# A two-layer decoder trunk: first conditioning strips loaded by feature half, and half of the first projections ahead of the second half

## What is computed

```
mod = silu(c) @ w_ada[0] + b_ada[0]           # 1024 -> 6 x 1024: shift1, scale1, gate1, shift2, scale2, gate2
h   = x * (1 + scale1) + shift1
z   = h @ w_in[0]                             # columns: 256 c_q | 128 c_kv | 64 k_rope | 512 gate_b | 512 gate_c | 512 u
q, k, v from rms_norm(c_q), rms_norm(c_kv), rope -> causal attention (4 heads)
conv = gate_b * causal_conv3(gate_c * u)
y   = concat(rms_norm(attn), rms_norm(conv)) @ w_o[0]
x   = layer_norm(alpha * x + gate1 * y)
```

## Time and profile before

| | us |
|---|---|
| median of three runs | 1417.23 (1416.96 to 1418.35) |
| profiled execution, first to last instruction (its span) | 1415.7 |
| what the median has beside that span | 1.5 |
| PE busy | 1390.7 (98%) |
| DVE busy | 1251.7 (88%) |
| ACT busy | 1012.6 (72%) |
| DMA | 482.16 MB, mean 341 GB/s |

### The profile page before, as it was taken

One profiled execution on the slowest core, in us unless ns is written; L12 is line 12 of the kernel. 1 busy time (PEld: TensorE's weight loads), 2 busy tenths in 40 slices (PEclk: granted clock), 3 DMA queues, 4 the chain that ended last, 5 costly groups with the idle time before them and its releaser, 6 DMA issues.

```text
span 1415.7 us, 20150 instructions
## 1 busy us (share of the span) xinstructions
PE 1390.7 (98%) x7013; PEld 1149.1 (81%) x7013; DVE 1251.7 (88%) x1388; ACT 1012.6 (72%) x1286; POOL 63.3 (4%) x123
## 2 busy tenths in 40 slices
PE   6999999999999999999999999999999999999996
PEld 4876999997967888888888888888888888888885
DVE  5987888876799989998998899999889899899998
ACT  2453544454355888888988888888898888888884
POOL 1000000000013500000000000000000000001000
PEclk9999999999999999999999999999999999999998
DMA  9996398977564999999999999999999999999970
GB/s 361 416 412 240 143 349 290 378 282 276 207 258 171 385 369 366 392 380 375 379 393 365 366 398 367 380 383 387 367 379 392 365 371 392 387 362 390 413 306 32
DMA packets 203472, 482.16 MB, mean 341 GB/s; under 512 B 6944, under 2 KB 31630, under 8 KB 203418
## 3 DMA queue, kind: packets, MB, share of 16 engines
q1 hardware_dynamic: 198848, 470.31, 88.1%
q0 software_dynamic: 1584, 5.77, 1.0%
q10 hardware_dynamic: 2986, 5.38, 1.0%
HBM read 475.67 MB, written 5.77 MB: 340 GB/s over the span
## 4 chain that ended last, share of the span: by engine, by line
PE 96%; DVE 2%; DMA 1%; ACT 0%; issue 0%; POOL 0%; SPq 0%; ACTq 0%; DVEq 0%; POOLq 0%
PE ps L1794 27%; PE ps L1796 27%; PE ps L1795 27%; PE ps L1957 2%; PE ps L2144 2%; PE ps L1815 2%; PE ps L1918 2%; PE ps L1971 1%; PE ps L1756 1%; DMA raw<-in_w_ada_dram 1%; PE ps L1731 1%; PE ps L1867 0%; PE ps L2094 0%; PE ps L1773 0%; PE ps L1729 0%; PE ps L1898 0%
## 5 line engine op out<-in xcount | busy, mean ns | idle before, releaser
L1424 DVE TENSOR_TENSOR low<-raw,w_hi 128x1024 fp32r<-128x1024 f32 x448 | 531.6, 1218 | 24.4 <-ACT w_hi L853 16.2
L853 ACT ACTIVATE w_hi<-raw 128x1024 fp32r<-128x1024 f32 x448 | 470.2, 1061 | 84.3 <-PE ps L1796 79.4
L1795 PE MATMUL ps<-low,h_hi 128*128 128x512 f32 x904 | 351.9, 389 | 0.0
L1794 PE MATMUL ps<-w_hi,h_lo 128*128 128x512 f32 x680 | 269.5, 396 | 0.0
L1796 PE MATMUL ps<-w_hi,h_hi 128*128 128x512 f32 x680 | 265.3, 390 | 0.0
L1795 PE MATMUL ps<-low,hid_hi 128*128 128x512 f32 x528 | 205.7, 390 | 0.0
L1795 PEld LDWEIGHTS ps<-low,h_hi 128*128 128x128 f32 x904 | 169.9, 188 | 34.2
L1424 DVE TENSOR_TENSOR low<-raw,e_hi 128x1024 fp32r<-128x1024 f32 x112 | 136.7, 1220 | 19.8 <-ACT e_hi L853 19.8
L1796 PEld LDWEIGHTS ps<-w_hi,h_hi 128*128 128x128 f32 x680 | 127.6, 188 | 27.4
L1794 PEld LDWEIGHTS ps<-w_hi,h_lo 128*128 128x128 f32 x680 | 127.8, 188 | 24.9
L1424 DVE TENSOR_TENSOR low<-raw,hx_lo 128x1024 fp32r<-128x1024 f32 x112 | 136.5, 1219 | 3.7
(11 more groups left out here) (377 smaller groups left out, 2268.0 us busy)
## 6 DMA issues: line engine op xcount, KB each, us to landing
raw<-in_moe_w_gate_dram SPq DMA_DIRECT2D x56, 2048.0 KB, 8.5
raw<-in_moe_w_up_dram SPq DMA_DIRECT2D x56, 2048.0 KB, 8.6
raw<-in_moe_w_down_dram SPq DMA_DIRECT2D x56, 2048.0 KB, 8.7
raw<-in_w_ada_dram SPq DMA_DIRECT2D x20, 2048.0 KB, 12.7
raw<-in_w_in_dram SPq DMA_DIRECT2D x6, 2048.0 KB, 12.5
raw<-in_ffn_w_gate_dram SPq DMA_DIRECT2D x11, 1024.0 KB, 8.3
raw<-in_ffn_w_up_dram SPq DMA_DIRECT2D x11, 1024.0 KB, 10.9
raw<-in_ffn_w_down_dram SPq DMA_DIRECT2D x11, 1024.0 KB, 4.9
```

What stands on the lines that cost most here:

```text
L853: act.activation(e_hi[k % ERING], raw[moe_slot(m)][:, (k % 4) * UNIT:(k % 4 + 1) * UNIT], ACT.Copy).then_inc(unit_hi, 1)
L1424: dve.tensor_tensor(low[moe_slot(m)][:, part], raw[moe_slot(m)][:, part], e_hi[k % ERING].bitcast(F32), ALU.subtract).then_inc(unit_lo, 1)
L1794: pe.matmul(o, x_lo, hi, start=first, stop=False, skip_group_check=True)
L1795: pe.matmul(o, x_hi, lo, start=False, stop=False, skip_group_check=True)
```

## The change

1. **c from rows.** `c` was loaded as a column per partition with 1024 elements of 4 bytes. It is now 8 rows of 128, and the first 2048 values of `b_ada` are 16 more; PE turns the 24 rows at once, ACT takes the Silu and two bias tables from PSUM.
2. **Strips by feature half.** The first four strips now hold 512 rows of 512 shift columns beside the same 512 scale columns. Strips 0 and 1 give shift and scale of features 0 to 511, strips 2 and 3 those of the rest. New order of the loads: strips 0, 1, first half of `x`'s columns, first half of `wa`'s rows, of `wb`'s rows, second half of `x`, strips 2, 3, second halves of `wa` and `wb`, `wc`, strips 4, 5, `wu`, strip 6, `qkv`, strip 7, `oc`, strip 8, `oa`, strip 9.
3. **PE** does the last chunk of all four strips itself. Its order is now: turn the 24 rows, `early_rows(0)`, three unread matmuls (eight before), `early_rows(1)`, turn the first half of `x`, `early_sums(0)`, `wa` over chunks 0 to 3, units 0 and 1 of gate_b, `early_rows(2)`, `early_rows(3)`, turn the second half, `early_sums(1)`, `wa` over chunks 4 to 7, turn the parameter rows, units 2 and 3.
4. **ACT and DVE** follow; DVE writes `modc` now. ACT's copy of the turned parameters stands ahead of unit 2, its Sin behind the root, DVE's angle table behind unit 4.
5. **Later strips.** Strips 4 to 6 are summed in the first projections (12 passes, all behind unit 5), 7 to 9 behind them (12 passes; before 4 to 7 and 8 to 9, four of the first 16 ahead of unit 3). The turns of vector 3 move from the attention scores to the convolution rows, and their bank 7 uses behind `ssq_conv`.

The core of the diff:

```diff
-BANK7 += [("ada", 0, 2, 0), ("ada", 0, 2, 1), ("ada", 0, 3, 0), ("ada", 0, 3, 1), ("ssq_conv", 0), ("ssq_attn", 0), ...
+EARLY_PE = ((3,), (3,), (3,), (3,))
+BANK7 += [("ada", 0, 2, 0), ("ada", 0, 2, 1), ("ssq_conv", 0), ("ada", 0, 3, 0), ("ada", 0, 3, 1), ("ssq_attn", 0), ...
-MIX_FIRST, MIX_LATE = ((4, 5, 6, 7), (9,)), ((8, 9), (10, 11))
+MIX_FIRST, MIX_LATE = ((4, 5, 6), (9,)), ((7, 8, 9), (10, 11))
...
+        def early_src(half, kh):
+            src = a["w_ada"][0][kh * 512:(kh + 1) * 512, 0:2 * D].rearrange("(c p) (v n) -> p c v n", p=P, v=2)
+            return src[:, :, :, half * 512:(half + 1) * 512]
...   (SP)
-            sp.dma_start(c_col[:, :], a["c"].rearrange("a (k p) -> p (a k)", p=P),
+            sp.dma_start(first_rows[0:KC, :], a["c"].rearrange("a (k p) -> (a k) p", p=P)).then_inc(c_loaded, 16)
+            sp.dma_start(first_rows[KC:3 * KC, :], a["b_ada"][0:1, 0:2 * D].rearrange("a (k p) -> (a k) p", p=P)).then_inc(c_loaded, 16)
...   (ACT, mixer)
                 halve(0)
+                unit(0)
+                unit(1)
+                if l == 0:
+                    act.wait_ge(bias_loaded, 16)
+                    ada_init(2)
+                    modulate_first(1)
+                halve(1)
                 if l == 0:
                     act.wait_ge(bank7_full, bank7("params") + 1)
                     act.activation(prm[:, :], ps[:, 7, 0:PRM], ACT.Copy).then_inc(bank7_free, 1)
-                unit(0)
-                unit(1)
-                halve(1)
+                unit(2)
                 if l == 0:
+                    unit(3)
+                    unit(4)
                     ada_init(3)
-                    act.wait_ge(angles, 1)
-                    act.activation(trig[:, :, :, :], ang[:, :, :, :], ACT.Sin).then_inc(trig_ready, 1)
-                unit(2)
...   (ACT: squares and root stand here)
-                for n in range(3, 6):
+                for n in range(5 if l == 0 else 3, 6):
                     unit(n)
+                if l == 0:
+                    act.wait_ge(angles, 1)
+                    act.activation(trig[:, :, :, :], ang[:, :, :, :], ACT.Sin).then_inc(trig_ready, 1)
...   (DVE)
+            def modulate_first(half):
+                use, cols = bank7(("ada", 0, half, 0)), slice(4 * half, 4 * half + 4)
+                dve.wait_ge(c_ready, 2)
+                dve.wait_ge(bank7_full, use + 1)
+                dve.tensor_tensor(modc[:, 0, 0:2, cols], ps[:, 7, 0:KC].rearrange("p (v k) -> p v k", v=2), bias_cols[:, :, cols],
+                                  ALU.add).then_inc(bank7_free, 1)
+                dve.wait_ge(bank7_free, use + 1)
+                dve.wait_ge(xt_mm, TT * (KC // 2) * (half + 1))
+                for c in (4 * half + 2, 4 * half + 3):
+                    dve.tensor_scalar(h_t[:, c, :], first_turned(c), modc[:, 0, 1, c:c + 1],
+                                      modc[:, 0, 0, c:c + 1], ALU.mult, ALU.add).then_inc(ht2_ready, 1)
...   (DVE, units 5 to 11)
-                    if l == 0 and n == MIX_UNITS - 1:
-                        sums(first, 2)
-                    elif l == 0 or n >= 9:
+                    if l == 0:
+                        sums(first, (0, 2, 1, 2, 2, 2, 2)[n - 5])
+                    elif n >= 9:
                         sums(first, 1)
...   (PE)
+            early_rows(0, True)
+            unread(3, 0)
+            early_rows(1, False)
+            turn_first(0)
             early_sums(0)
...
+                if l == 0:
+                    for t in range(TT):
+                        compressed(t, 0, KC // 2)
+                    channels(0, 0, (0, 1))
+                    use_bank7(("ada", 0, 1, 0))
+                    early_rows(2, True)
+                    early_rows(3, False)
+                    turn_first(1)
+                    early_sums(1)
+                    wait_load(pe, ("wa", 0))
+                    for t in range(TT):
+                        compressed(t, KC // 2, KC).then_inc(za_mm, 1)
+                    use_bank7("params")
+                    pe.wait_ge(prm_loaded, 16 * PRM_LOADS)
+                    pe.transpose(ps[:, 7, 0:PRM], prm_rows[:, :], ident[0:PRM, 0:PRM]).then_inc(bank7_full, 1)
+                    channels(0, 0, (2, 3))
```

More of the change, by code:

```diff
@@ L489, in _ @@
                     sp.wait_ge(s, value)
[L490 to L495, removed]
+                for q in range(len(loads[n][1])):
+                    load_part(n, q)
             def expert_loads(i, e, first, store):
@@ L671, in modulate @@
             def modulate(v, l, row, last, t):
[L673 to L678, removed]
+                act.wait_ge(fold_ready, v)
+                shift, scale = modf[:, v, 0, :], modf[:, v, 1, :]
                 tok = slice(t * P, (t + 1) * P)
-                for c in range(KC) if v >= 1 and t == 0 else ACT_C:
+                for c in range(KC) if t == 0 else ACT_C:
                     act.wait_ge(xt_mm, TT * KC * v + KC * t + (c | 3) + 1)
@@ L1134, in _ @@
             dve.wait_ge(c_ready, 1)
-            for n in range(4):
-                ada(0, n)
+            ada(0, 0)
+            ada(0, 1)
             def residual(k, t):
@@ L1208, in sums @@
                         ada_part(l, v, c, c + 1)
+                halve(0)
+                unit(0)
+                unit(1)
                 if l == 0:
-                    sums(first, 4)
+                    ada(0, 2)
+                    ada(0, 3)
+                    modulate_first(1)
+                halve(1)
+                unit(2)
                 unit(3)
                 unit(4)
+                if l == 0:
+                    angle_table()
                 dve.wait_ge(rms_ready, l + 1)
@@ L1807, in mixer, with compressed @@
                 wa = slot_of(("wa", l))[:, 0:KC * ZA].rearrange("p (c n) -> p c n", c=KC)
-                for t in range(TT):
-                    for n, c in enumerate(range(KC)):
-                        if l == 0 and t == 0 and c == KC // 2:
-                            wait_load(pe, ("wa", l))
-                        if l == 1 and t == 0 and n == 6:
+                def compressed(t, first, last):
+                    for c in range(first, last):
+                        if l == 1 and t == 0 and c == 6:
                             turn_input(2, 1)
@@ L1815, in mixer, with channels @@
                         m = pe.matmul(ps[:, 4 + t, 0:ZA], h_t[:, c, t * P:(t + 1) * P], wa[:, c, :],
-                                      start=(n == 0), stop=(n == KC - 1))
-                    m.then_inc(za_mm, 1)
-                def channels(first, bank):
-                    for k in range(4):
+                                      start=(c == 0), stop=(c == KC - 1))
+                    return m
+                def channels(first, bank, ks=range(4)):
+                    for k in ks:
                         name, at, g = mix_weight(l, first + k)
```

286 lines of the change are left out of this document (167 added, 119 removed).

## The result

The changed kernel takes 1431.24 us (median of four runs, 1430.47 to 1431.87) against 1417.1 (1416.9 to 1418.35) of the kernel before on the same chip: ratio 1.0096, interval 1.0084 to 1.0109, so 14.1 us slower. The profiled execution has a span of 1430.1 us against 1415.7, 14.4 more. The page of the kernel after, to be set against the earlier trace rows: PE is busy 8.4 us longer (time at half clock counts as busy) and the chain gives more to DVE and ACT.

A forecast was written before the change was run, and what follows sets the result against it. PE was taken to bound the kernel, busy 98% of the span. Terms -10.0 + 7.1 + 4.8 + 2.9 + 2.6 + 1.2 = +8.6 us on 1417.2 gave 1425.8 us; own range 1422 to 1430, full range 1416.9 to 1432.5.

The forecast's parts named there:

- (a): Opening: strip 0 lands at about 9.7 us and the first `wa` matmul starts at 23.2 instead of 33.2; -10.0 us.
- (b): Between the `wa` halves: one-column records, turns, sums and `modc` now stand on PE, their data not late; +7.1 us.
- (c): Both low stretches: each `wa` half restarts at half clock, 2.0 us each, plus 0.8 in the second's sums; +4.8 us.
- (d): Behind `wa`: ACT's parameter copy ahead of unit 2 makes units 2 to 4 late and PE idle; +2.9 us.
- (e): Unit 5 and behind: ACT's late root and Sin, and DVE's units and passes, make PE wait; +2.6 us.
- (f): Before the attention sum: PE waits for ACT's row block copy and drain of vector 3's second half; +1.2 us.
- the rival on that: Opening: the clock doesn't come up in the three unread matmuls; 4.4 us more, 1430.2 us, to 1433; chance 0.15.
- one of its own signs: Prediction wrong if the output projection starts later by another amount than the kernel's end.
- the clock holds: Rival: no fall to half clock in the low stretches, so (c) is 0 and the time 1421.0 us; chance 0.18.
- The head start is kept: Rival: (d), (e) and (f) are hidden and the clock holds, so the time is 1414.3 us; chance 0.09.

The follow-up runs named there:

- the first experiment: Changed kernel with ACT's copy of the turned parameters moved behind units 2 to 4: 1430.12 us, ratio 1.0081.
- The last experiment: The dense opening with 12 DVE conditioning passes left out (vectors 2 to 4 of layer 0 come out wrong): 1415.53 us, ratio 0.9983.
- The third experiment: Changed kernel with the attention's sum of squares ahead of vector 3's second half in bank 7: 1431.33 us, ratio 1.0091.
- the dense opening: The one with all three, with DVE summing all early chunks and PE running five unread matmuls first, three between turns and sums of the second half: 1419.84 us.
- The best complete kernels here, 1419.49 and 1419.84: 1419.84 us is the dense opening; 1419.49 us is the same without the three unread matmuls between the halves.
- the kernel with the first two edits: Changed kernel with parameters copied behind units 2 to 4 and DVE doing the last chunks of strips 2 and 3: 1423.01 us, ratio 1.0041.
- the one with all three: The kernel with the first two edits plus the bank 7 order of the third experiment: 1420.83 us, ratio 1.0020.
- the first two dense ones: The dense opening, 1419.84 us, and the same without its three unread matmuls between the halves, 1419.49 us.
- The dense kernel with the changed order of bank 7: The dense opening with the changed kernel's bank 7 order instead of the third experiment's: 1421.33 us, ratio 1.0023.

## Why the prediction was right, and where its sizes were off

The forecast was 1425.8 us, slower; it came out slower at 1431.24, inside the range given and above the forecast's own range of 1422 to 1430. The mechanism is the one forecast; the term that was mis-sized is the clock in the opening, 4.8 us where 8.2 were measured. On the profiled execution:

| step | forecast | measured | from |
|---|---|---|---|
| (a) first half earlier, clock apart | -10.0 | -8.6 | 25.70 against 33.21, and 1.1 of it clock |
| (b) inserted, at full clock | +7.1 | +7.2 | 39.92 to 48.89, less 1.8 |
| (c) clock in both low stretches | +4.8 | +8.2 | 1.1 + 1.8 + 5.25 |
| (d) parameters' copy | +2.9 | +2.7 | 57.71 to PE's next record at 60.45 |
| (e) unit 5 and behind | +2.6 | +2.5 | `wa`'s end to u's end, 36.37 for ten units; before 36.92 for twelve, less 5.75 for two; less (d) |
| (f) bank 7 | +1.2 | +1.1 | 11.9 to 13.0 |
| clock in the router | none | +1.3 | 13.0 to 14.3 |
| sum | +8.6 | +14.4 | span: +14.4 |

(a) The first strip landed at 10.58, not 9.7. I had read the small column load as 1.2 us of DMA time in its way. It is gone, and the strip lands no earlier than before (10.35 then); moving the parameters' loads away brought no gain that could be seen. In the chain its transfer starts 1.20 us later than before (3.14 against 1.94, behind more issues on SP) and takes 0.97 less. Whether the later issue ate the gain is untested, and what sets the landing stays open. The 1.1 us of clock in the table are 0.6 in the unread matmuls, which took 5.33 us where I had 4.7 (the full rate came only at their end, so the rival on that was nearly right), and 0.5 in the sums (2.27 for 1.8).

(b) The count of instructions was right. The data were not late, and PE went from unit 1 to the one-column records without a gap.

(c) This is the term that was mis-sized. I let each half start with some 4 us at half clock. The second had been at half for the turns and sums in front (1.28 and 3.22 us where 0.9 and 1.8 would do) and stayed there until 54.1. The two halves of `wa` took 8.47 and 8.82 us; 12.04 / 2 is 6.02 each. My upper bound for them was 2.7 each, so this part (5.25) lay just inside it. What I had sized too low was the clock's price on the low work itself (0.8 in all, where 1.1 and 1.8 were measured), and I had left out the falls further on. An idle gap of 2.65 us, which step (d) makes, was followed by one (60.9 to 64.3 us). It took 1.7 us in unit 2 and so moved gate_b's end, but by the chain it isn't in u's end, where DVE sets the pace.

(d) Right, and shown by the first experiment, where ACT makes units 2 to 4 before 54 us, beside `wa`.

(e) Right, in mechanism and size. DVE's last low part of u ends 33.1 us behind `wa` (90.85 against 57.71); the forecast's 8.8 and 25.1 make 33.9. Counted from gate_b's end, the stretch grew by 0.7 only (26.1 against 25.4), since the clock in unit 2 had made gate_b itself late. Without that fall PE would by the chain have waited longer for DVE instead; no run takes the fall away and leaves the rest as it is. One detail was wrong: the root was done at 65.03, 7.3 us behind `wa`, and DVE took it up at 66.35 because its own angle table, which the forecast had not counted, stood first (62.58 to 66.35). The last experiment shows the price of the passes where PE is early. The load of the Sin table took 1.28 us (66.17), and the Sin ran right behind it at 67.46. The estimate by the Trainium skill ("ScalarE: Activation LUTs", section "What ACT_TABLE_LOAD costs"), 1.4 more, is not borne out: the trace shows no drain between the two.

(f) Right: PE stands 1.98 us from 128.66 to 130.64 behind ACT's `yv` and drain. The third experiment adds that DVE comes next: there PE waits 0.97 us for its last pass.

By one of its own signs the prediction was off: the output projection starts 13.0 us later and the kernel ends 14.4 later, where the two should have been equal. What lies between is the fall in the router (1.3), which the sum didn't have.

Of the rivals, "the clock holds" fell at 23.3 us, in a row with PE busy throughout; the Trainium skill's rule ("TensorE: Matmul & The Clock Gate", section "What's actually happening"), taken as busy time, fell with it in two places of this kernel. "The head start is kept" is what the dense opening tries to be. It keeps the start but meets DVE's waits and passes, and ends 0.14% above the kernel before.

So the change loses in this way: the time gained, 7.5 us, is paid back by 9.0 us of conditioning that now stands on PE in the middle of the projections; the rest is 6.3 us behind three choices in the order of instructions (d, e and f) and 6.6 us of half clock in `wa` and the router, beside 2.9 that stand in the other two numbers. The best complete kernels here, 1419.49 and 1419.84, are level with the kernel before (1.0009, interval 0.9999 to 1.0018) and just above it (1.0014); none beats it.

## What to carry to other kernels

An early start on the bounding engine is worth only what the work that must still come between costs less than it; count that work first, at the clock that it will have. When work that was done while an engine waited is moved behind the start, it needs a new place on another engine as well: here DVE's passes came to stand where DVE was already busy 22.9 of 25 us (57 to 82, kernel before). Before a copy is put into an engine's order, look which instruction of the other engine releases it, and what stands behind it.

## What the hardware showed that I had not expected

- The granted clock fell while PE was 1.00 busy with one-column records, turns and sums (23.3 and 43.8 us), and it also fell within 1 us behind short gaps (60.9 in this kernel, behind 2.65 us; 128.2 in the first experiment, behind 1.98). A fall cost from 1.3 us (the router) to 4.6 (turns, sums and the second half of `wa`).
- Executions of one kernel differ by amounts the size of falls, and the slower ones show a lower mean clock: 0.995 of full at 1419.77 us and 0.990 at 1425.22 for the kernel with the first two edits. That kernel, the one with all three and the first two dense ones spread over 4.6 to 5.5 us (1416.94 to 1421.87 for the dense opening), where the kernel before spreads over 2.3 (1416.63 to 1418.91) beside them. The dense kernel with the changed order of bank 7 spreads over 1.9 only. One profiled execution can hide a gain of this size, so the starts of rows told more than the spans.
- At the start the column of the granted clock reads 1.00 while PE runs at half speed. In this stretch of the kernel after there are 6 one-column records, where the stretch at 20 us has 11:

```profile
13.00:14.00 1.00, 1.00 (x6) 1.00 (x6) 0.71 (x1) 0.00 (x0) 0.00 (x0) 1.00 1.06 410
```
